# Routing of a mixture-of-experts layer: ranks and the first gathering of rows with fp32r operands in two parts

## What is computed

```python
def moe_swiglu(h, w_r, b_r, w_g, w_u, w_d):
    t = h.reshape(B * S, D)
    logits = jnp.dot(t, w_r) + b_r
    top_v, top_i = lax.top_k(logits, TOP_K)
    top_w = jax.nn.softmax(top_v, axis=-1)
    gates = jnp.sum(jax.nn.one_hot(top_i, N_EXPERTS) * top_w[..., None], axis=1)
    for e in range(N_EXPERTS):
        out = out + gates[:, e:e + 1] * swiglu(t, w_g[e], w_u[e], w_d[e])
```

## Time and profile before

| | |
|---|---|
| time, three runs | median 1334.82 us (1334.12, 1334.82, 1335.08) |
| the profiled execution | 1333.96 us, its span 1332.4 us, 1.6 us around it |
| PE busy | 1312.0 us, 98% of the span |
| DVE, ACT, POOL busy | 1012.8, 833.8, 82.0 us |
| mean granted clock of PE | 0.995 of 2.4 GHz |
| data moved | 386.18 MB, mean 290 GB/s |

### The profile page before, as it was taken

One profiled execution on the slowest core, in us unless ns is written; L12 is line 12 of the kernel. 1 busy time (PEld: TensorE's weight loads), 2 busy tenths in 40 slices (PEclk: granted clock), 3 DMA queues, 4 the chain that ended last, 5 costly groups with the idle time before them and its releaser, 6 DMA issues.

```text
span 1332.4 us, 17842 instructions
## 1 busy us (share of the span) xinstructions
PE 1312.0 (98%) x6725; PEld 1122.4 (84%) x6725; DVE 1012.8 (76%) x778; ACT 833.8 (63%) x747; POOL 82.0 (6%) x105
## 2 busy tenths in 40 slices
PE   7999999999999999999999999999999999999998
PEld 6998888888889888888888888888888888888886
DVE  5758765444465777688888888888889888888987
ACT  5546554444455545477777677677677777767674
POOL 4200110000012010100000000000000000000100
PEclk9999999999999999899999999999999999999999
DMA  8633435655598235199999899899999998999994
GB/s 304 205 107 122 153 111 189 205 189 189 190 348 301 96 126 193 60 382 389 335 408 389 340 415 371 352 408 353 375 391 347 399 388 334 415 378 344 413 406 172
DMA packets 117002, 386.18 MB, mean 290 GB/s; under 512 B 6256, under 2 KB 33500, under 8 KB 116956
## 3 DMA queue, kind: packets, MB, share of 16 engines
q1 hardware_dynamic: 105068, 365.09, 72.7%
q0 software_dynamic: 3168, 11.54, 2.2%
q10 hardware_dynamic: 8720, 8.91, 1.9%
HBM read 369.79 MB, written 15.73 MB: 289 GB/s over the span
## 4 chain that ended last, share of the span: by engine, by line
PE 89%; DVE 6%; ACT 1%; issue 1%; DMA 1%; SPq 0%; POOL 0%; DVEq 0%; ACTq 0%
PE bank L1656 36%; PE bank L1652 25%; PE bank L1653 25%; DVE wl L1145 2%; PE bank L2218 1%; DVE wl L1159 1%; DVE scratch L1292 1%; DMA ring<-in_we_gate 1%; DVE scratch L1270 1%; PE bank L1833 0%; PE bank L1675 0%; DVE aT_low L1164 0%; ACT wh L798 0%; PE bank L2107 0%; DMA scratch<-in_g_k 0%
## 5 line engine op out<-in xcount | busy, mean ns | idle before, releaser
L1159 DVE TENSOR_TENSOR wl<-ring,wh 128x2816 fp32r<-128x2816 f32 (+1 forms) x127 | 400.1, 3171 | 53.3 <-PE bank L1656 38.7
L798 ACT ACTIVATE wh<-ring 128x2816 fp32r<-128x2816 f32 (+1 forms) x128 | 336.9, 2633 | 139.6 <-PE bank L1653 44.5
L1145 DVE TENSOR_TENSOR wl<-ring,wh 128x2048 fp32r<-128x2048 f32 (+3 forms) x79 | 188.2, 2382 | 121.3 <-ACT wh L784 120.7
L1652 PE MATMUL bank<-wh,xh 128*128 128x512 f32 (+1 forms) x696 | 264.6, 380 | 1.2 <-DVE wl L1159 0.6
L1653 PE MATMUL bank<-wh,xl 128*128 128x512 f32 (+1 forms) x696 | 263.1, 378 | 0.0
L1656 PE MATMUL bank<-wl,xh 128*128 128x512 f32 (+1 forms) x944 | 241.8, 378 | 0.0
L784 ACT ACTIVATE wh<-ring 128x2048 fp32r<-128x2048 f32 (+2 forms) x78 | 154.7, 1984 | 119.8 <-PE bank L1653 101.5
L1159 DVE TENSOR_TENSOR wl<-ring,wh_third 128x2816 fp32r<-128x2816 f32 (+1 forms) x64 | 187.1, 2923 | 28.2 <-PE bank L1656 25.5
L1656 PEld LDWEIGHTS bank<-wl,xh 128*128 128x128 f32 x944 | 174.8, 188 | 25.4
L798 ACT ACTIVATE wh_third<-ring 128x2816 fp32r<-128x2816 f32 (+1 forms) x64 | 155.5, 2430 | 33.5 <-DMA ring<-in_we_up 14.1
L1652 PEld LDWEIGHTS bank<-wh,xh 128*128 128x128 f32 x696 | 130.6, 188 | 27.3 <-issue 1.9
(11 more groups left out here) (258 smaller groups left out, 1576.2 us busy)
## 6 DMA issues: line engine op xcount, KB each, us to landing
ring<-in_we_gate SPq DMA_DIRECT2D x64, 1408.0 KB, 7.4
ring<-in_we_up SPq DMA_DIRECT2D x64, 1408.0 KB, 8.2
ring<-in_we_down SPq DMA_DIRECT2D x56, 1536.0 KB, 8.7
ring<-in_w_in SPq DMA_DIRECT2D x8, 1536.0 KB, 11.2
ring<-in_w_in SPq DMA_DIRECT2D x10, 1024.0 KB, 5.6
ring<-in_w_gate SPq DMA_DIRECT2D x10, 1024.0 KB, 5.1
ring<-in_w_up SPq DMA_DIRECT2D x10, 1024.0 KB, 5.0
ring<-in_w_down SPq DMA_DIRECT2D x10, 1024.0 KB, 4.8
```

What stands on the lines that cost most here:

```text
L798: nc.scalar.activation(wh_in_pass(j, n), ring[:, slot, 0:n], ACT.Copy).then_inc(high_ready, 1)
L1145: nc.vector.tensor_tensor(wl[:, j, 0:n], ring[:, slot, 0:n], wh[:, j, 0:n].bitcast(F32), ALU.subtract).then_inc(low_ready, 1)
L1159: nc.vector.tensor_tensor(wl[:, j % 2, 0:n], ring[:, pass_slot(j), 0:n], wh_in_pass(j, n).bitcast(F32), ALU.subtract).then_inc(low_ready, 1)
L1652: nc.tensor.matmul(dst, x_high, w_high, start=first, stop=False)
```

## The change

The ranks and the first gathering take fp32r operands, of which PE does a product in one pair of load and product. The choice (`either`), the triangle (`tri8r`, a copy that POOL makes at the kernel's start) and the 0/1 places (`with_row`) are exact in fp32r. The scaled rows are not, so they come in two parts: ACT writes `rows_high` (two instructions of 1024 columns), DVE writes `rows_low` with `rows_split`, one tile before the slot number is made and one after `with_row`. The gathering has a product with each part: 32 fp32r products where there were 16 float32 ones. The exact `xrows`, which the scatter needs, are now made by POOL, after its iota. In the choice the instructions of the two token tiles stand side by side, with one wait for both. DVE's order after the routing becomes: `gathered_low` of ga0, low part of fill 0, low part of fill 1, `gathered_low` of ga1, the gate weights, low part of fill 2. In the loop the low part of the next pass's fill 1 moves from the head of a pass to the end of the one before. Three of the results change their banks (rank1, ga0, ga1), so that the first products of fills 0 and 1 do not use the banks that ga0 and ga1 are in.

```diff
--- before.py
+++ after.py
@@ -146,10 +146,8 @@
             for q in range(4):
                 plan.add((l, f"d{q}"), plan.next(4 + q))
         else:
-            for n, b in (("r", 4), ("rank0", 5), ("rank1", 6)):
+            for n, b in (("r", 4), ("rank0", 5), ("rank1", 3), ("ga0", 7), ("ga1", 6)):
                 plan.add((l, n), b)
-            plan.add((l, "ga0"), 1)
-            plan.add((l, "ga1"), 3)
     loop_base = list(plan.uses)
     in_pass = PsumPlan()
     HBLOCKS = [(0, 4), (4, 4), (8, 3)]
@@ -260,6 +258,9 @@
         with nc.sbuf_tensor("wh_third", [P, SLOT], F32R) as wh_third:
             with nc.sbuf_tensor("row_spare", [P, D], F32) as row_spare:
                 pass
+        with nc.sbuf_tensor("rows_high", [P, TT, D], F32R) as rows_high:
+            with nc.sbuf_tensor("rows_low", [P, TT, D], F32R) as rows_low:
+                pass
         aT_low = sb("aT_low", [P, KT, S], F32R)
         with nc.sbuf_tensor("hT", [P, KT, S], F32) as hT:
             pass
@@ -317,6 +318,7 @@
         group_low = [al[:, i * 4 * S:(i + 1) * 4 * S] for i in range(2)]
         h1 = ffn[:, 0:DFF]
         oneh = ffn[:, DFF:DFF + 256].rearrange("p (t s) -> p t s", t=TT)
+        with_row = sb("with_row", [P, TT, PASS_CAP], F32R)
         place = ffn[:, DFF + 256:DFF + 256 + PASS_CAP]
         gated = ffn[:, DFF + 384:DFF + 640].rearrange("p (t s) -> p t s", t=TT)
         gatedT = ffn[:, DFF:DFF + 256]
@@ -328,6 +330,7 @@
 
         ident = sb("ident", [P, P])
         tri8 = sb("tri8", [P, S])
+        tri8r = sb("tri8r", [P, S], F32R)
         crow = sb("crow", [P, 3 * P], F32R)
         pick32 = sb("pick32", [P, FH])
         pick = sb("pick", [P, FH], F32R)
@@ -669,6 +675,7 @@
             select(pick32[:], [[-1, FH]], ALU.not_equal, -1.0, -HD, 1)
             then_wait(select(spreadg[:], [[-1, 8 * P]], ALU.is_ge, 0.0, HD - 1, HD))
             nc.gpsimd.tensor_copy(pick[:], pick32[:])
+            nc.gpsimd.tensor_copy(tri8r[:], tri8[:])
             nc.gpsimd.memset(mcv_rows[:], 0.0)
             nc.gpsimd.memset(zeros[:], 0.0)
             nc.gpsimd.iota(first[:], [[PASS_CAP, NE]], base=-1, channel_multiplier=0,
@@ -720,6 +727,8 @@
             pool.wait_ge(rstd_ready, RSTDS[L - 1, "ffn"])
             nc.gpsimd.iota(place, [[1, PASS_CAP]], base=0, channel_multiplier=0,
                            allow_small_or_imprecise_dtypes=True).then_inc(place_ready, 1)
+            for t in range(TT):
+                nc.gpsimd.tensor_scalar(xrows[t], xres[:, t, :], msq[:, 4 + t:5 + t], None, ALU.mult).then_inc(xn_ready, 1)
             pool.wait_ge(rows_chosen, 1)
             pool.wait_ge(xn_ready, XN[L - 1, "ffn"])
             for t in range(TT):
@@ -1036,6 +1045,9 @@
                         if (nm, i, s) == ("d", NG - 2, 0):
                             hidden_high(NG - 1)
                 else:
+                    act.wait_ge(rstd_ready, RSTDS[l, "ffn"])
+                    for t in range(TT):
+                        nc.scalar.activation(rows_high[:, t, :], xres[:, t, :], ACT.Copy, scale=msq[:, 4 + t:5 + t]).then_inc(rhigh_ready, 1)
                     act.wait_ge(topd_ready, 1)
                     nc.scalar.activation(gw[:, :, 1:2], gw[:, :, 0:1], ACT.Exp).then_inc(tope_ready, 1)
 
@@ -1473,16 +1485,21 @@
                                                      ALU.mult, ALU.add)
             ins.then_inc(take(l, "r"), 1)
             dve.wait_ge(*taken(l, "r"))
-            for t in range(TT):
-                then_wait(nc.vector.max(top[:, t, :], logit[:, t, :]))
-                then_wait(nc.vector.max_index(topi[:, t, :], top[:, t, :], logit[:, t, :]))
+            nc.vector.max(top[:, 0, :], logit[:, 0, :])
+            then_wait(nc.vector.max(top[:, 1, :], logit[:, 1, :]))
+            nc.vector.max_index(topi[:, 0, :], top[:, 0, :], logit[:, 0, :])
+            then_wait(nc.vector.max_index(topi[:, 1, :], top[:, 1, :], logit[:, 1, :]))
             then_wait(nc.vector.tensor_copy(topf[:], topi[:]))
-            then_wait(nc.vector.tensor_tensor(hot[:, :, 0:2, :], eight[:].unsqueeze(1).unsqueeze(1).to_broadcast([P, TT, 2, NE]),
+            then_wait(nc.vector.tensor_tensor(hot[:], eight[:].unsqueeze(1).unsqueeze(1).to_broadcast([P, TT, 2, NE]),
                                               bcast_last(topf[:, :, 0:2], NE), ALU.is_equal))
-            nc.vector.tensor_tensor(hot[:, :, 2, :], hot[:, :, 0, :], hot[:, :, 1, :], ALU.add).then_inc(sel_ready, 1)
+            nc.vector.tensor_tensor(either[:], hot[:, :, 0, :], hot[:, :, 1, :], ALU.add).then_inc(sel_ready, 1)
             nc.vector.tensor_tensor(gw[:, :, 0:1], top[:, :, 1:2], top[:, :, 0:1], ALU.subtract).then_inc(topd_ready, 1)
-            for t in range(TT):
-                nc.vector.tensor_scalar(xrows[t], xres[:, t, :], msq[:, 4 + t:5 + t], None, ALU.mult).then_inc(xn_ready, 1)
+
+            def rows_split(t):
+                dve.wait_ge(rhigh_ready, t + 1)
+                act_low(rows_low[:, t, :], xres[:, t, :], rows_high[:, t, :], msq[:, 4 + t:5 + t]).then_inc(rlow_ready, 1)
+
+            rows_split(0)
             dve.wait_ge(sel_ready, 1)
             dve.wait_ge(*full(l, "rank0"))
             rank = bank(l, "rank0")[:, 0:TT * NE].rearrange("p (t e) -> p t e", t=TT)
@@ -1490,13 +1507,15 @@
                                                      ALU.mult, ALU.add))
             dve.wait_ge(place_ready, 1)
             for t in range(TT):
-                ins = nc.vector.tensor_scalar(oneh[:, t, :], place, slot[:, t, 0:1], hot[:, t, 2, 0:1], ALU.is_equal, ALU.mult)
+                ins = nc.vector.tensor_scalar(with_row[:, t, :], place, slot[:, t, 0:1], either[:, t, 0:1].bitcast(F32),
+                                              ALU.is_equal, ALU.mult)
             ins.then_inc(oneh_ready, 1)
+            rows_split(1)
             nc.vector.tensor_scalar(later[:], rank, 8.0 * PASS_CAP, float((NE - 1) * PASS_CAP), ALU.is_gt, ALU.mult
                                     ).then_inc(take(l, "rank0"), 1)
             dve.wait_ge(*taken(l, "rank0"))
             then_wait(nc.vector.tensor_tensor(slot[:], slot[:], later[:], ALU.add))
-            then_wait(nc.vector.tensor_tensor(picked[:], hot[:, :, 0:2, :], slot[:].unsqueeze(2).to_broadcast([P, TT, 2, NE]),
+            then_wait(nc.vector.tensor_tensor(picked[:], hot[:], slot[:].unsqueeze(2).to_broadcast([P, TT, 2, NE]),
                                               ALU.mult))
             then_wait(nc.vector.tensor_reduce(rowf[:], picked[:], AX_X, ALU.add))
             nc.vector.tensor_copy(rows[:], rowf[:]).then_inc(rows_chosen, 1)
@@ -1510,8 +1529,8 @@
             highs0 = HIGHS["passes"]
             PASS_HIGHS = FB + 2
 
-            def gathered_low(count, bank_, take_):
-                for i in range(2):
+            def gathered_low(count, bank_, take_, banks=range(2)):
+                for i in banks:
                     dve.wait_ge(acthigh_ready, count + i)
                     for k in range(4):
                         c = 4 * i + k
@@ -1519,15 +1538,17 @@
                                       col(L - 1, "ffn", c))
                     ins.then_inc(take_(f"ga{i}"), 1)
 
+            gathered_low(highs0 + 1, lambda n: bank(L - 1, n), lambda n: take(L - 1, n), range(1))
             dve.wait_ge(high_ready, NSPLIT + 1)
             dve.wait_ge(*pe_done_static(split_names[-2]))
             low(pass_slot(0), fill_width(0), 0)
-            dve.wait_ge(tope_ready, 1)
-            then_wait(nc.vector.tensor_scalar(gw[:, :, 2:3], gw[:, :, 1:2], 1.0, None, ALU.add))
-            then_wait(nc.vector.reciprocal(gw[:, :, 2:3], gw[:, :, 2:3]))
-            then_wait(nc.vector.tensor_tensor(gw[:, :, 3:4], gw[:, :, 1:2], gw[:, :, 2:3], ALU.mult))
-            gathered_low(highs0 + 1, lambda n: bank(L - 1, n), lambda n: take(L - 1, n))
-
+
+
+            def gate_weights():
+                dve.wait_ge(tope_ready, 1)
+                then_wait(nc.vector.tensor_scalar(gw[:, :, 2:3], gw[:, :, 1:2], 1.0, None, ALU.add))
+                then_wait(nc.vector.reciprocal(gw[:, :, 2:3], gw[:, :, 2:3]))
+                then_wait(nc.vector.tensor_tensor(gw[:, :, 3:4], gw[:, :, 1:2], gw[:, :, 2:3], ALU.mult))
 
             def last_rows():
                 then_wait(nc.vector.tensor_scalar(cnt[:, 1:2], cnt[:, 0:1], 8.0 * PASS_CAP, float(NE * PASS_CAP), ALU.is_gt, ALU.mult))
@@ -1547,8 +1568,11 @@
 
             dve.wait_ge(route_ready, 1)
             rounds = dve.value_load(npass[0:1, 0:1], min_val=1, max_val=2)
+            low_in_pass(1, 0)
+            gathered_low(highs0 + 1, lambda n: bank(L - 1, n), lambda n: take(L - 1, n), range(1, 2))
+            gate_weights()
+
             def expert_pass(p, e, last):
-                low_in_pass(1, p)
 
                 def lows(*slots):
                     for j in slots:
@@ -1606,7 +1630,7 @@
                     rows_added(0, 0)
                 else:
                     gathered_low(p * PASS_HIGHS + (highs0 + 2 + FB + 1), lbank, ltake)
```

(21 more changed lines are left out.)

5 lines of the change are left out of this document (4 added, 1 removed).

## The result

| | before | after |
|---|---|---|
| median | 1335.43 us (20 runs, 1334.12 to 1337.66) | 1337.19 us (20 runs, 1336.08 to 1341.78) |
| ratio of after to before | | 1.0017, 95% interval 1.0011 to 1.0023 |
| profiled execution | 1333.96 us | 1341.78 us |

The change makes the kernel 1.76 us slower at the medians; by the ratio in the table it is 2.3 us. The whole interval lies above no change. The ratio is inside the 0.2% that I called the same, though the interval's upper end does not. The forecast was 1336.7 us, in a range from 1333.0 to 1338.5. Three executions further down were disturbed (two of e8_warm at 1447 us, one of the kernel before at 5166 us); the ratios leave them out. One caution comes first: the execution that was profiled is the slowest of the 20. Its order of events can be read, its length can't.

The account below looks back on a forecast made before the run. PE, busy 1312.0 of 1332.4 us, was the bound. Zero to the places, gathering +0.5, clock +1.7, a 0.2 us wait gone: +1.9 on 1333.96 gives 1335.9; the median's 0.86 more gives 1336.7 us, range 1333.0 to 1338.5.

Parts of the forecast that it names:

- the sum: Terms up to PE's start of fill 2, at 577.25 instead of 575.33: +1.9 us, taken as the kernel's loss.
- POOL's copies: POOL makes `xrows` from 555.45 in two copies of 1.04 us, at most 1.8 us each, ending at 557.6.
- The hold-up of DVE: In the choice, two-input `hot` and `either` wait until POOL's copies end: +0.35 us.
- Choice and ranks: Before the gathering: choice -0.2 us, ranks -0.65 us, but `rows_split(0)` delays the slot number, +0.5 us.
- Price of a pair: In the gathering, a one-pass pair still costs 0.213 us at half clock, its weight load being the price.
- Rival 2: One-pass gathering pairs are priced by columns, 0.115 us each: 1333.5 us, -1.3 us; chance 0.18.
- From the gathering to the pass: PE reaches the first pass 0.75 us after the last gathering pair's start, 0.5 us late at 567.65.
- The clock: Gathering pairs don't restore full clock; it returns 3.4 us into the first pass, at 571.05: +1.7 us.
- Rival 1: The clock returns in the gathering as before, at 565.7; fill 2's low part costs +0.75 us: 1335.6 us; chance 0.20.
- DVE's order: In the first pass, moved low parts stay hidden, fill 2's only because PE is late; fill 6 costs 0 to 0.3 us.
- Loads and scatter: POOL's scatters, queued behind its copies, wait for the row numbers until 562 anyway and are hidden.

Follow-up runs that it names:

- e8_warm: e6 plus dense dummy products of 384 columns in PE's idle time, five after the router and three after the ranks: 1334.34 us, 0.9992.
- e7: The kernel after without its four scatters, so later passes don't get their rows; POOL's copies stay: 1336.14 us, 1.0010.
- e3: The kernel after with DVE's gate weights and reading of ga1 moved ahead of the low part of fill 1: 1335.18 us, 1.0002.
- e4: The kernel after without the gathering's products with `rows_low`, 16 pairs instead of 32; PE still waits for `rows_low`: 1335.40 us, 0.9998.
- e2: The kernel after with PE gathering POOL's `xrows` in float32 operands again; the two parts are still made: 1337.51 us, 1.0015.
- e10: e3 plus dense dummy products of 384 columns in PE's idle time, nine after the router and four after the ranks: 1335.99 us, 1.0008.
- e1: The kernel after with POOL's two copies moved behind its wait for the row numbers, in front of the scatter: 1338.51 us, 1.0026.
- e5: e3 with `xrows` made by ACT behind `rows_high`, POOL making none: 1335.47 us, 1.0002.
- e6: The kernel before with only the fp32r ranks and the choice's paired waits: 1333.81 us, 0.9990.
- e9: The kernel after with the float32 gathering of before, DVE making `xrows` and POOL copying nothing; new order and banks kept: 1334.83 us, 1.0002.
- e12: The kernel before without its four scatters, so later passes don't get their rows; control for e7: 1335.56 us, 1.0002.

## Why the prediction was right, and where it wasn't

The forecast was right in time and sign, and partly by luck. At fill 2 it had +1.9 us; after's profile has +2.25 and e7's +0.7 (21.67 and 20.11 against 19.42 after the logit). After's +2.25 came with two errors that largely cancel: the gathering began 1.0 us later than before, where I had no delay, and the pass began 0.22 us after the last pair's start, where I had 0.75. And the measured loss has a part that the sum held to be hidden, PE's wait for the low part of fill 2, which adds 0.85 us in after and 1.3 in e7.

- **POOL's copies: size wrong.** I took 1.04 us each, with 1.84 as the upper bound. They take 2.85 (2.87 and 3.16 in four other profiles), outside my bounds. The failed step was to price a TENSOR_SCALAR by a row of another operation. Even the dearest of POOL's rows, 1.8 us for 1024 columns with two inputs, lay below it.
- **The hold-up of DVE: mechanism only half right.** I had DVE's two-input steps wait until POOL's instruction had ended. In after's profile the CAST, which has one input, took 1.01 us and ended at 558.29, when POOL's first copy had ended at 558.26. `hot` took 1.08 us and ended 1.7 us before POOL's second copy did. `rows_split(0)`, with two inputs, took its normal 1.28 us beside a copy. In e3, e4, e2 and e7 only the places were held up, 1.19 us instead of 0.60. So the price is 0.6 us in four profiles and 1.7 in two (after and e10, which have the same end of the CAST). In those two the logit started 0.8 us after POOL's first copy, in the four 0.35. Had `hot` stood still until the second copy ended at 561.09, it would have been 3.6 us. The Trainium skill ("SBUF — State Buffer", section Who interferes with whom), which I had cited for this, has the ports held for a whole instruction. The CAST's end fits that; `hot`, the places and `rows_split(0)` don't. The place of the steps against POOL's copies goes with which step is hit, but no run varied it by itself, so what decides it stays open.
- **Choice and ranks: right.** The steps gave 0.3 us (`hot` starts 1.28 us after the logit in e3, 1.56 in before), and five pairs took 1.23 us. The slot number waited for the end of `rows_split(0)` and not for the bank, as forecast. Where POOL isn't in the way (e1, e5) the gathering begins 0.7 us earlier than in before; I had bounded that at 0.5. e6 is faster by 0.1% than before: these two edits were the good ones.
- **Price of a pair: right.** 0.213 us with one-pass products, with float32 ones, and with half as many (e4). Rival 2, the price by columns, is out. The Trainium skill's 107 ns a load ("TensorE: Matmul & The Clock Gate", section LDWEIGHTS), which I had set beside it, isn't met at half clock.
- **From the gathering to the pass: too dear.** I carried over the 0.75 us that lay between the last pair's start and the pass in before, where PE waited 0.47 us for DVE. With ga0 read ahead of the low part of fill 0 it was 0.22 us in after. The gathering itself got 0.6 us longer, near the 0.5 that I had.
- **The clock: right.** I had it back 3.4 us into the pass; it was 3.5 in after's profile, and 2.4 to 4.3 in the seven profiles with one-pass pairs in the gathering. Fill 0 took 5.51 us where 3.93 stood: +1.58 for a forecast 1.7 (+1.1 in e3 and e7). Rival 1 is out. The loss in fill 0 is partly made good at once: the waiting in fill 1 goes, as forecast, and with it 0.4 us of fill 1 (4.23 us in before, 3.83 in after) and not 0.2, so that e3 is only 0.6 us behind before at fill 2 and measurably not slower. So PE's slow time is in part time in which it would have waited for DVE.
- **DVE's order: the wrong step.** I wrote that the low part of fill 2 would be "hidden only because PE is late" and that fill 6 would cost 0 to 0.3 us. It isn't hidden: PE waits for it in all the profiles that have this order and the full gathering, 0.57 us in after, 1.01 in e1, 1.18 in e2, 1.03 in e7 and 0.59 in e9. I had the low part of fill 2 start at 575.8; it started at 577.68. The two causes are the low part of fill 1, which waited for ACT until 572.40 and not until 570.95, and a gap of 0.68 us between the gate weights and the low part of fill 2. That gap is in all six profiles in which the small steps stand right ahead of the loop (after, e1, e2, e4, e7, e9), and in neither e3 nor e5, where a step of 3.1 us does; I take it for the entry into the loop, which was not tested. From the late low part the loads of fills 6 and on start late (3.9 us at fill 6). I had also left out that SP waits for the low part of fill 0, which I had moved behind ga0: the load of fill 4 starts 5.2 us later. In e3 it is 4.1 us later too and costs nothing measurable, so it isn't the loss by itself. e3, which alters only this order, gives back 0.0015 in the ratio, 2.0 us. This is about the whole loss (0.0017). What is left in e3, the clock, the gathering and POOL together, then costs about what the choice, the ranks and the earlier reading of ga0 bring; no run has the clock's part by itself.
- **Loads and scatter: a link I had left out.** I called the scatters hidden. In after they run from 564 to 578.7 beside loads that the new order has made late. Without them after is about 1 us faster (e7), while before isn't (e12), and putting them later still costs more (e1). The loads beside them take longer: that of fill 5, until ACT could read it, 6.6 us without and 8.3 with them, 10.1 in e1. The differences in time are of the size of the intervals, so the slower loads are shown, and their part of the time is likely rather than shown; the 2.76 us wait in e1 is its clearest sign.

## What to carry to other kernels

A step that is late by x costs x only where nothing else is late: ask of every moved step where its engine idled before and whether it now stands behind the next step that somebody waits for. A three-line exchange of DVE's order gave back 0.0015 of the ratio here; the best of the arithmetic edits (e6) won 0.0010. Products of 128 columns or fewer were priced by their weight loads here (0.21 to 0.22 us a pair at half clock, for 8 columns as for 128), so fewer passes in each gain nothing where the number of pairs stays the same (gathering); they gain where it falls (ranks, ten to five). Take a price for an engine from the same operation on that engine, or leave the bound open above. Before moving a step, list everyone who waits for it, the queue that issues the loads included.
